# Order of the weight splits, of one operand split and of two products at the start of a feed-forward stage

## The reference

```python
def conv_ffn(h, w_up, conv_w, conv_b, w_down):     # h (1, 1024, 1024), w_up (1024, 2 * 2816)
    u = h @ w_up
    pad = CONV_WIDTH // 2                          # CONV_WIDTH = 3
    u = lax.conv_general_dilated(
        u, conv_w[:, None, :].astype(u.dtype), window_strides=(1,), padding=((pad, pad),),
        dimension_numbers=('NWC', 'WIO', 'NWC'), feature_group_count=2 * D_FF) + conv_b
    g, val = jnp.split(u, 2, axis=-1)
    return (jax.nn.silu(g) * val) @ w_down         # w_down (2816, 1024)
```

## Time and profile before

| | us |
|---|---|
| median of 3 runs | 2880.34 (2877.79 to 2882.91) |
| the profiled execution | 2876.81 |
| its span, first to last instruction | 2875.0 |
| mean granted TensorE clock | 0.982 |
| TensorE busy | 2745.5 (95%) |
| VectorE busy | 1783.1 (62%) |
| GpSimd busy | 1470.1 (51%) |
| ScalarE busy | 1357.7 (47%) |

### The profile page before, as it was taken

How to read it: one execution, slowest core, us unless ns; L and a number is a source line. 1 busy time by engine, 2 the same in 40 slices (tenths; PEclk the granted TensorE clock), 3 DMA queues, 4 the chain that set the end, 5 groups by cost and what they waited for, 6 DMA issues and landing times. The chain is left out here.

```text
span 2875.0 us, 40322 instructions
## 1 busy us (share of the span) xinstructions
PE 2745.5 (95%) x13708; PEld 2309.3 (80%) x13708; DVE 1783.1 (62%) x2490; ACT 1357.7 (47%) x2109; POOL 1470.1 (51%) x1128
## 2 busy tenths in 40 slices
PE   6999999998989999999989999998899999999998
PEld 5788888887878888788868888887787788887886
DVE  7477777773565544555578888887627445545555
ACT  4477777773344444321246665665414444442212
POOL 4255555543587777544543333332226877774443
PEclk9999999999999999999999999999899999999998
DMA  3000000003212222522020000000430212225221
GB/s 129 30 8 8 10 9 7 3 16 132 74 66 88 88 88 71 212 90 96 36 112 23 30 30 31 30 23 8 162 102 30 103 73 88 88 75 218 88 88 59
DMA packets 54392, 195.35 MB, mean 68 GB/s; under 512 B 6544, under 2 KB 9872, under 8 KB 53776
## 3 DMA queue, kind: packets, MB, share of 16 engines
q1 hardware_dynamic: 54288, 193.95, 18.5%
HBM read 148.84 MB, written 45.09 MB: 67 GB/s over the span
## 5 line engine op out<-in xcount | busy, mean ns | idle before, releaser
L1207 PE MATMUL ffn_ps<-ffn_b_hi,weights_hi 128*128 128x512 f32 x704 | 278.5, 396 | 18.4 <-POOL weights_lo L718 10.0
L1208 PE MATMUL ffn_ps<-ffn_b_lo,weights_hi 128*128 128x512 f32 x704 | 277.2, 394 | 0.0
L1209 PE MATMUL ffn_ps<-ffn_b_hi,weights_lo 128*128 128x512 f32 x704 | 276.9, 393 | 0.0
L358 POOL TENSOR_TENSOR weights_lo<-weights_raw,weights_hi 128x1024 fp32r<-128x1024 f32 (+2 forms) x67 | 132.5, 1982 | 224.5 <-ACT weights_hi L353 224.4
L1098 POOL TENSOR_TENSOR ffn_y_lo<-ffn_y_raw,ffn_y_hi 128x1024 fp32r<-128x1024 f32 x44 | 109.1, 2497 | 230.9 <-ACT ffn_y_hi L1028 230.9
L718 POOL TENSOR_TENSOR up_local_lo<-up_sums,up_local_hi 128x512 fp32r<-128x512 f32 x126 | 171.1, 1361 | 96.9 <-ACT up_local_hi L713 96.9
L2227 ACT ACTIVATE dif_p<-dif_s,dif_neg_max 128x1024 f32<-128x1024 f32 x128 | 142.2, 1114 | 121.2 <-DVE dif_neg_max L2414 110.3
L1207 PE MATMUL ffn_ps<-ffn_b_hi,up_local_hi 128*128 128x512 f32 x504 | 196.3, 389 | 0.0
L1208 PE MATMUL ffn_ps<-ffn_b_lo,up_local_hi 128*128 128x512 f32 x504 | 196.3, 389 | 0.0
L1209 PE MATMUL ffn_ps<-ffn_b_hi,up_local_lo 128*128 128x512 f32 x504 | 196.1, 389 | 0.0
L1028 ACT ACTIVATE ffn_y_hi<-ffn_y_raw 128x1024 fp32r<-128x1024 f32 x44 | 44.2, 1052 | 315.0 <-PE ffn_ps L1209 315.0
(11 more groups left out here) (343 smaller groups left out, 8543.4 us busy)
## 6 DMA issues: line engine op xcount, KB each, us to landing
weights_raw<-in_up SPq DMA_DIRECT2D x44, 512.0 KB, 3.6
up_raw<-in_up SPq DMA_DIRECT2D x44, 512.0 KB, 4.2
ffn_products<-ffn_conv SPq DMA_DIRECT2D x44, 512.0 KB, 2.7
ffn_y_raw<-ffn_products SPq DMA_DIRECT2D x44, 512.0 KB, 4.0
ffn_down_raw<-in_down SPq DMA_DIRECT2D x24, 512.0 KB, 6.4
weights_raw<-in_diff_qkv SPq DMA_DIRECT2D x23, 512.0 KB, 3.5
weights_raw<-in_down SPq DMA_DIRECT2D x20, 512.0 KB, 5.8
x_spill<-x_in SPq DMA_DIRECT2D x16, 512.0 KB, 4.3
```

Of the source, the lines that this page charges most:

```text
L358: pool.tensor_tensor(w.lo[:], w.raw[:], w.hi[:].bitcast(F32), ALU.subtract).then_inc(w.lo_done, 1)
L1207: pe.matmul(out, hi, x_hi, start=start, stop=False, skip_group_check=True)
L1208: pe.matmul(out, hi, x_lo, start=False, stop=False, skip_group_check=True)
L1209: return pe.matmul(out, lo, x_hi, start=False, stop=stop, skip_group_check=True)
```

## The change

In cycle 1 ScalarE makes the `hi` of S3(1) before T3's instead of at the start of the cycle, then the `hi` of A11, S4 of pair 2, A22 of pair 1 and A12 of pair 2, and only then the silu, T4's `hi`, S2 and S1. GpSimd makes T4's `lo` after those of A22(1) and A12(2) instead of before. On TensorE, P2(2) comes before P4(1) instead of after, and `product_no` is changed to match. Other cycles are as before. No instruction is added or removed.

```diff
--- before.py
+++ after.py
@@ -644,6 +644,8 @@
 
     if isinstance(p, int) and p == 1 and name in ("P1", "P3"):
         return 5 if name == "P1" else 6
+    if isinstance(p, int) and (p, name) in ((2, "P2"), (1, "P4")):
+        return 13 if p == 2 else 14
     if isinstance(p, int) and p == PAIRS - 1 and name == "P4":
         return 7 * p + 4
     return 7 * p + {"P1": -3, "P3": -2, "P4": 6, "P2": 0, "P6": 1, "P5": 2, "P7": 3}[name]
@@ -975,23 +977,34 @@
 
             centre(0, 0, 0)
             copy_first(1, 1)
+            act.wait_ge(summed, 4)
+            block_high(act, blocks, 1, 1, "S3")
             t_high(T3)
             act.wait_ge(prod, 4)
             centre(1, 0, 0)
 
             def cycle(p, par, m):
-                act.wait_ge(summed, 4 * p)
-                need(act, prod, free(p, "S3"))
-                block_high(act, blocks, p, par, "S3")
-
                 begin = isinstance(p, int) and p == 1
                 if not begin:
+                    act.wait_ge(summed, 4 * p)
+                    need(act, prod, free(p, "S3"))
+                    block_high(act, blocks, p, par, "S3")
                     copy_first(par, p)
+                else:
+                    act.wait_ge(raw_loaded[0], 32)
+                    act.wait_ge(prod, free(2, "A11"))
+                    block_high(act, blocks, 2, 0, "A11")
+                    act.wait_ge(summed, 7)
+                    act.wait_ge(prod, free(2, "S4"))
+                    block_high(act, blocks, 2, 0, "S4")
+                    block_high(act, blocks, 1, 1, "A22")
+                    act.wait_ge(prod, free(2, "A12"))
+                    block_high(act, blocks, 2, 0, "A12")
 
                 act.wait_ge(conv_done[0], p)
                 act.activation(conv[:, 0, :], conv[:, 0, :], ACT.Silu).then_inc(silu_done, 1)
 
-                if not is_last(p):
+                if not is_last(p) and not begin:
                     act.wait_ge(raw_loaded[1 - par], 32 * m)
                     need(act, prod, free(p + 1, "A11"))
                     block_high(act, blocks, p + 1, 1 - par, "A11")
@@ -1001,10 +1014,9 @@
 
                 if begin:
                     t_high(T4)
-                need(act, prod, free(p, "A22"))
-                block_high(act, blocks, p, par, "A22")
-
-                if not begin:
+                else:
+                    need(act, prod, free(p, "A22"))
+                    block_high(act, blocks, p, par, "A22")
                     act.wait_ge(c21_done, p - 1)
                     act.wait_ge(y_stored, 16 * p - 16)
                     centre(1, p - 1, 1 - par)
@@ -1013,7 +1025,7 @@
                     down_high_y(0, 0, 1)
                     down_high_w(0, 0, 1)
                 else:
-                    for name in ("A12", "S2", "S1"):
+                    for name in ("S2", "S1") if begin else ("A12", "S2", "S1"):
                         need(act, prod, free(p + 1, name))
                         block_high(act, blocks, p + 1, 1 - par, name)
 
@@ -1083,11 +1095,12 @@
                     add_sums(pool, blocks, p + 1, 1 - par, 32 * m)
                     block_low(pool, blocks, p + 1, 1 - par, "A11")
                     block_low(pool, blocks, p + 1, 1 - par, "S4")
-                if isinstance(p, int) and p == 1:
-                    t_low(T4)
                 block_low(pool, blocks, p, par, "A22")
                 if not is_last(p):
-                    for name in ("A12", "S2", "S1"):
+                    block_low(pool, blocks, p + 1, 1 - par, "A12")
+                    if isinstance(p, int) and p == 1:
+                        t_low(T4)
+                    for name in ("S2", "S1"):
                         block_low(pool, blocks, p + 1, 1 - par, name)
 
             cycles(pool, cycle)
@@ -1250,10 +1263,13 @@
                     pe.wait_ge(conv_done[0], p - 1)
                 product(p, "A11", BANK_A[par], B11, stop=False)
                 product(p, "S4", BANK_C[par], B22)
-                if not first:
+                second = isinstance(p, int) and p == 2
+                if not first and not second:
                     fourth(p - 1)
                 pe.wait_ge(s1_done, p)
                 product(p, "A12", BANK_A[par], B21, start=False)
+                if second:
+                    fourth(p - 1)
                 if first:
                     pe.wait_ge(t_hi, 4)
                     pe.wait_ge(t_lo_dve, 2)
```

## The result

The changed kernel takes 2883.18 us, median of 12 runs (2879.72 to 2886.30); the kernel before, beside it, 2877.50 (12 runs, 2874.35 to 2882.91). The ratio is 1.0019, 95% interval 1.0012 to 1.0027: 5.5 us slower, between 3.5 and 7.8. The profiled execution took 2882.53, its span is 2880.6 (2875.0 before).

The account below looks back on a forecast made before the run. TensorE's products wait for GpSimd's `lo` parts, 10.0 us in 4 pauses, in cycle 2. Per copy −0.2 + 2.2 (clock) = +2.0, two copies +4.0: 2880.8 from the profiled execution, 2884.3 from the median; range 2877 to 2889.3.

Parts of the forecast that it names:

- Steps 1 and 2: Cycle 1: early S3(1) `hi` costs ScalarE nothing; GpSimd, alternating with VectorE, gains 1.5 us, VectorE loses 3.2 us.
- Step 3: Convolutions on VectorE end later, so P7(1) starts at 801.79, a new TensorE wait of 2.8 us.
- Step 4: Weight splits ahead of the silu cost ScalarE nothing; the 2.33 us wait is gone, P1(2) starts at 804.64.
- step 7: Half clock on TensorE after the long pause costs 2.2 us per copy, between 0 and 2.8.
- Step 5: T4 later on VectorE; GpSimd's sum S3(2) ends at 816.95 against 818.14, a gain of only 1.2 us.
- Step 6: Swapped products: TensorE stands 8.07 us before P2(2); P1(3) moves by −0.21 at full clock, −0.17 in the second copy.
- GpSimd's lead: Rival: turns cost less, GpSimd's 4.3 us head start carries through, −5.7 per copy, 2869 to 2874; chance 0.10.
- The clock was down: Rival: half clock holds over P2(2) and P4(1), 7 to 10 us of work; 2886.5 to 2889.3; chance 0.20.
- VectorE did not keep its turn: Rival: VectorE's step 2 subtractions run through, GpSimd's last sum at 817.5, +0.55 per copy more, 2885.4; chance 0.06.
- the swap alone counts: Rival: split orders don't bite, P2(2) stays at 819.34, P1(3) +3.2 per copy, 2886.7; chance 0.06.

Follow-up runs that it names:

- e3: The kernel before with the `hi` of S3(1) made ahead of T3's and nothing else; ratio 1.0012, +3.5 us.
- e2: The kernel before with only P2(2) and P4(1) of cycle 2 swapped; ratio 1.0013, +3.7 us.
- e5: The changed kernel with ScalarE's copy of P1(2) moved to the end of cycle 1, ahead of the centre tap; ratio 1.0016, +4.6 us.
- e9: As e5, and the value centre tap of pair 1 right behind the silu of cycle 2; ratio to the kernel before 0.9969, -8.9 us.
- e1: The changed kernel with P4(1) before P2(2) again, split orders as changed; ratio to the kernel before 0.9984, -4.6 us.
- e4: The changed kernel with 24 additional matmuls filling TensorE's pause ahead of P2(2); ratio to the kernel before 0.9992, -2.3 us.
- e12: As e1, with the value centre tap of cycle 2 right behind the silu; ratio to the kernel before 0.9978, -6.3 us.
- e10: As e9, with P4(1) before P2(2) again; ratio to the kernel before 0.9979, -6.0 us.

## Why the prediction was right

The forecast was +4.0 us on the kernel before, between 2877.0 and 2889.3; measured +5.5. That 2884.3 stands so near to 2883.18 is partly luck: the median of before was 2.8 us lower over 12 runs than over the 3 shown.

- *Steps 1 and 2* (turns). Right to a tenth: with 0.36 for the start of the stage, T3's last `lo` ends at 799.59 − 0.36 = 799.2, forecast 799.21; the last sum ends at 800.72 − 0.36 = 800.36, forecast 800.36. In e3 the early S3(1) does it alone.
- *Step 3* (P7(1) late). Forecast 801.79, measured 802.32 − 0.36 = 801.96.
- *Step 4* (splits ahead of the silu). Right: no wait before P1(2). P7(1) ran partly at half clock and took 4.0 us, which step 7 named and which costs nothing.
- *Step 5* (T4, sum S3(2)). First stage: forecast 816.95, measured 817.32 − 0.36 = 816.96. Second stage: the sum ends 1.1 us later than forecast. GpSimd and VectorE, changed kernel:

```profile
2222.57 2.28 POOL L720 TENSOR_TENSOR weights_lo<-weights_raw,weights_hi 128x512 fp32r<-128x512 f32 x1
2224.87 6.63 POOL L1080 TENSOR_TENSOR ffn_b_lo<-x_in,ffn_b_hi 128x1024 fp32r<-128x1024 f32 x2
...
2221.34 4.59 DVE L1154 TENSOR_TENSOR x_in<-x_in 128x1024 f32<-128x1024 f32 x2
...
2225.86 3.43 DVE L1179 TENSOR_TENSOR ffn_conv<-ffn_conv 128x1024 f32<-128x1024 f32 x1
```

  There T4's two subtractions take 4.59 instead of 3.38 and the two `lo` of GpSimd 6.63 instead of 5.71, because each finds the other at work once more. P2(2) starts at 2236.38 where 2232.46 + 2.81 (how much later P1(1) of this stage is than before) = 2235.3 was forecast. Behind it stands the late beginning, GpSimd 2.3 us later behind P1(1) before any moved step. e2, whose splits are those of before, has it too and its P2(2) is 1.1 us later than before. In the second stages of e5 and e9, whose splits of cycle 1 are the changed ones, the stage begins as before and the sum S3(2) ends 32.2 and 31.9 us behind P1(1), where 32.1 was forecast. So the replay took the second stage to begin as in the profile of before, and in this profile it did not; why stages begin in two ways stays open.
- *Step 6* (the swap). Right in place and sign. e1 and e2 show it from both sides: taken out it gives back 3.7 and 3.0 us up to cycle 3, put in alone it costs 3.1 and 3.7. The pause was 6.15 and 7.22 us instead of 8.07, since P7(1) and P1(2) before it were slower; its end stood in the first stage (32.74 behind P1(1), forecast 32.73).
- *Step 7* (clock). From P2(2) to P1(3) it took 16.41 and 15.82 us where 13.73 is full clock: 2.7 and 2.1, forecast 2.2, range 0 to 2.8. They fit the 5.8 and 4.4 us of products at half clock, of which 0.46 is lost. e4 shows the term by itself: 2.7 and 2.1 us less with the pause filled.

The sum per stage is −0.2 + 2.7 = 2.5 in the first, and −0.2 + 1.1 + 2.1 = 3.0 in the second. What the sum missed is the 1.1 of the second stage's late beginning, which starts ahead of every step that the edit moves and need not be in every execution, and 0.5 of the first stage's clock. That the places add up to just the 5.5 of the medians is luck in part too, for in other runs the two differ by up to 4.

Of the rivals, GpSimd's lead did not carry (e3, and the sum 1.2 us early, not 3). The clock was down for 5.8 us behind the restart and for 4.4 in the second stage, not 7. VectorE did not keep its turn (4.55 for two). That the swap alone counts falls with e1: the split orders move P1(3) by −1.2 in the first stage. What I had not seen is what does make the stage shorter: the centre tap of the value part taken from behind the `hi` of S4(3) and so behind GpSimd's sum, 1.6 us in the first stage (e12 against e1). Taking the copy of P1(2) from behind its sum adds 0.6 there (e10 against e12). With both early the swap moves P1(3) forward by 3.1 us in the first stage (e9 against e10), but P7(3) gives nearly all of it back.

## What to carry to other kernels

Before two pieces of work are swapped to fill a wait, ask what each of them waits for: the one that goes first has to be the one that is ready first, and here it hung on a copy that stood in ScalarE's queue behind a split that waited for GpSimd. Replaying two cycles, with the turns that VectorE and GpSimd take read off a few rows, gave the places of the first stage to 0.2 us; what it missed was that the second stage can begin with GpSimd 2.3 us later. Look at how a stage begins before a difference of 1 us in it is put down to an edit, and follow the gain to where the pauses end: 2.4 us at one product was 0.1 a few products on (e9 against e10). Price a pause of TensorE with the slow time behind it, wherever the pause moves (e5).

## What was not expected of the hardware

The same pause in the same place can be followed by full or by half clock. In the first stage's down-projection TensorE stands 2.68 us in both kernels, far from the change. First the kernel before, restart and window, then the changed one:

```profile
1196.69 0.47 PE L1207 MATMUL ffn_ps<-ffn_y_hi,ffn_down_hi 128*128 128x512 f32 x1 [2.68 <-POOL ffn_down_lo L1104]
...
1196.00:1200.00 4.00, 3.31 (x15) 2.77 (x16) 1.25 (x1) 1.06 (x1) 0.55 (x1) 1.00 1.03 421
```

```profile
1199.54 0.57 PE L1220 MATMUL ffn_ps<-ffn_y_hi,ffn_down_hi 128*128 128x512 f32 x1 [2.68 <-POOL ffn_down_lo L1117]
...
1199.50:1203.00 3.50, 3.46 (x9) 2.74 (x10) 0.60 (x1) 1.06 (x1) 0.00 (x0) 0.54 1.03 420
```

The granted clock is 1.00 in one and 0.54 in the other, and 0.46 of these 3.5 us, 1.6, are lost. The last matmul of the up-projection comes 2.0 us behind the first one of its product in the first case, and 2.6 in the second, and the first one itself 7.0 and 8.1 behind the product before. Such differences, not of the edits' making, and the late beginnings fit the few us by which places and medians disagree in the table, though I didn't show that they are all of it.
